# Attention's probabilities turned by VectorE blocks and transfers, a later scan and convolution, and other orders at the seams, in a two-layer hybrid trunk

## The chip, the cores and the metric

The kernel runs on one core of a Trainium2 chip. The metric is the device time of one execution in microseconds, as the median of several runs. The core has a matrix engine (TensorE, PE in the profile, with its weight loads as PEld), VectorE (DVE), ScalarE (ACT), GpSimd (POOL) and SyncE (SP), which issues nearly all transfers here. The engines run side by side and wait for each other by semaphores. Operands lie in SBUF, products in the eight banks of PSUM.

## The reference

Each of two layers computes

```python
x = layer_norm(ALPHA * x + 0.5 * swiglu(x, ffn1...), ln1)
x = layer_norm(ALPHA * x + hybrid_mixer(x, ...), ln2)
x = layer_norm(ALPHA * x + 0.5 * swiglu(x, ffn2...), ln3)
```

on 256 tokens of 1024 features in float32, with 2816 hidden features. The mixer projects `x @ w_in` into the inputs of three branches and their 3 x 1024 gates:

```python
y_conv = (b_g * (conv3(c_g * h) + conv_b)) @ w_br_conv
s      = complex diagonal scan over time of B u;  y = gelu(C s + d u)
y_ssm  = (y * sigmoid(y @ w_glu)) @ w_br_ssm
p      = exp(scores - m) / (sum(exp(scores - m)) + exp(sink - m))   # window of 128
y_attn = (p @ v) @ w_br_attn                   # 8 query heads, 2 key heads, 2 blocks of 128
mix    = (g0 * y_conv + g1 * y_ssm + g2 * y_attn) @ w_out
```

## The kernel before, in words

**Products.** Every large product is made of three: an operand is split into a high part (ScalarE casts it to fp32r) and a low part (VectorE subtracts it), and high by high, high by low and low by high are added up in PSUM. The weights stream through three slots, `raw[0..2]` to `w_hi` and `w_lo`, one chunk of 128x2048 at a time: SP loads chunk k (`load`) once `lo_made` says that chunk k-3 is split, ScalarE makes `w_hi` (`split`), VectorE `w_lo` (`rest`, called `lo(k)` in the mixing stage), and TensorE's `take` waits for `lo_made` and gives the slot back with `used`. All engines follow orders that are written out by hand; there is no scheduler.

**FFN.** Eleven steps of gate and up products and of `down` products (`accumulate`, which adds into four banks: two token tiles by two halves of 512). The hidden rows are turned by `blocks_turned`, a VectorE transpose of 32x32 blocks, four transfers to DRAM and one back that puts the blocks in their places (`turn_hidden` on SP). The last step's hidden rows are turned by TensorE.

**Seams.** At a seam the residual sum, its variance and the normalisation (VectorE, with the power on POOL) of tile 0, then of tile 1 follow the last products; TensorE transposes the tile (`transposes`, 8 pieces), ScalarE scales it out of PSUM and casts it, VectorE subtracts the low part (`x_rest`), and the next stage's first products start on each pair of feature chunks as it is ready (`x_lo`). There are five: into each mixing stage, into each second FFN, and from layer 0 to layer 1. The next stage's first chunks are split ahead: `split_first` and `split_halves` on ScalarE, `rest_first` and `rest_halves` on VectorE. At the seam into the second FFN both halves of the low part stand ahead of the norm; at the other three VectorE makes them inside it. `transposes` of tile 0 stands between the two halves of the last `accumulate`.

**Mixing stage.** TensorE's order is: keys and queries, scores (`S1` for the second block of queries, 256 keys, `S0` for the first, 128 keys), state inputs, and five pairs of gate chunks, `gates_upper(p)` (chunk 9+2p) and `gates_lower(p)` (chunk 10+2p), each half a set of 24 products. Upper products of pair p+1 need the bank that ScalarE's `gate(p, t)` has read. Between them stand:

```python
gates_lower(0); transposes of the probabilities, 24 pieces
gates_upper(1); output_states(0); input_states(1); attend(1); gates_lower(1)
gates_upper(2); gates_lower(2); gates_upper(3); gates_lower(3); gates_upper(4)
attend(0); output_states(1); gates_lower(4)
```

ScalarE normalises the probabilities (`normalise`) and copies the turned ones from six banks to `probsT` (`probs_out`). `input_states` gives B u of a quarter of the states in PSUM, which ScalarE copies (`states`); VectorE turns it (`turn_in`), scans it (`scan`), turns it back (`turn_out`) and TensorE takes it in `output_states`, which needs two quarters. `states(2)` and `turn_in(2)` need `input_states(1)`. VectorE's order from `lo(11)` on is: scan(1), lo(12), turn_out(1), lo(13), convolution (six operations and a product), turn_in(2), lo(14), attn_rest, scan(2), lo(15), turn_out(2), lo(16), turn_in(3), lo(17), scan(3), turn_out(3), lo(18), and then the low parts of the branches.

Line 360 and line 364 issue the blocks' transfers, 334 the weights'; 544 to 546 are gate and up products, 567 `accumulate`, 580 `transposes`, 807 `input_states`, 817 `output_states`, 828 `transpose_probs`, 841 `attend`; 1376 is `rest`, 1413 the block transpose, 1740 to 1772 the turns, 1762 the scan, 1852 to 1857 the convolution, 1153 `gate`, 1161 `states`, 1477 to 1492 the norm, 1388 `rest_halves`.

Of the kernel before, what the change touches and what calls it, by code (L numbers as in the profile page):

```python
# [27 lines left out]
P = 128  # L28
# [71 lines left out]
def trunk(nc, x, ffn1_w_gate, ffn1_w_up, ffn1_w_down, ln1_g, ln1_b, w_in, conv_w, conv_b,  # L100
# [4 lines left out]
    with ctx:  # L105
# [3 lines left out]
        def overlay(first, second):  # L109
# [20 lines left out]
        probsT_first = gates[:, 5, :, :].rearrange("p t (h n) -> p (t h) n", n=P)  # L130
        probsT, rows_hi, rows_lo = overlay(
            [("probsT", [P, 2 * HEADS, P], F32)],
            [("rows_hi", [P, 2, 2, SEQ], F32R), ("rows_lo", [P, 2, 2, SEQ], F32R)])
        S1, y_attn = overlay([("S1", [P, HEADS, 2 * P], F32)], [("y_attn", [P, 4, 2, SEQ], F32R)])

        b_in = S1[:, 0, :].rearrange("p (r t c) -> p r t c", r=2, t=STATE_TILES)
# [57 lines left out]
        ps = ctx.enter_context(nc.psum_tensor("ps", [P, 8, 512], F32))  # L194
        hid_dram = nc.dram_tensor("hid_dram", (4, 32, 4, P), F32, kind="Internal").ap()
# [68 lines left out]
        pT_done = Events(sem("pT_done"), 6)  # L264
        pT_made = Events(sem("pT_made"), 6)
# [45 lines left out]
        def _(sp):  # L311
# [54 lines left out]
            def load_ffn(l, f, w_gate, w_up, w_down, after_two, after_steps, before_last):  # L366
# [14 lines left out]
                after_two()  # L381
                load(l, k0 + 4, rows(w_down, l, 0))

# [53 lines left out]
            for l in range(DEPTH):  # L437
# [18 lines left out]
                def nothing():  # L456
                    pass

                def vectors():

                    dma = sp.dma_start
                    dma(dt_rows[:, :], ssm_log_dt.rearrange("l (t g) -> (l t) g", g=2)).then_inc(small_landed, 16)
# [7 lines left out]
                    for n, v in enumerate((ln1_g, ln1_b, ln2_g, ln2_b, ln3_g, ln3_b)):  # L470
                        dma(ln_rows[16 * n:16 * n + 16, :],
                            v.rearrange("l (c p) -> (l c) p", p=P)).then_inc(small_landed, 16)
# [19 lines left out]
                def norm2():  # L492

                    sp.wait_ge(sum_made.sem, sum_made.at(l, 2))
                    load_norm(l, ln2_g, ln2_b)
# [17 lines left out]
        def _(pe):  # L513
# [43 lines left out]
            def accumulate(slot, buf, start=False, stop=False, tiles=range(NT), halves=((0, 1),)):  # L557
# [104 lines left out]
            def ffn(l, f, norm, turn):  # L662
# [64 lines left out]
                accumulate(2, 1, stop=True, tiles=(1,), halves=((0,),))  # L727
                turn()
                accumulate(2, 1, stop=True, tiles=(1,), halves=((1,),)).then_inc(used.sem, 1)

            for l in range(DEPTH):
# [65 lines left out]
                def input_states(g):  # L797

                    if g:
                        pe.wait_ge(bu_made.sem, bu_made.at(l, 2))  # L800
                        pe.wait_ge(pT_made.sem, pT_made.at(l, 4))
# [19 lines left out]
                def transpose_probs(S, parts, g0):  # L821

                    for g in range(parts):
                        b = (6, 7, 0, 1, 2, 3)[g0 + g]
                        for n in range(4):
                            i = 4 * g + n
                            src = S[:, i // 2, (i % 2) * P:(i % 2) * P + P] if parts == 4 else S[:, i, :]
                            last = nc.tensor.transpose(ps[:, b, n * P:n * P + P], src, ident[:, :])  # L828
                        last.then_inc(pT_done.sem, 1)

                def attend(blk):

                    pe.wait_ge(pT_made.sem, pT_made.at(l, 4 if blk else 6))
                    held = probsT if blk else probsT_first
# [52 lines left out]
                gates_lower(2)  # L887
                gates_upper(3)
# [68 lines left out]
                def output(j, tiles=range(NT), halves=((0, 1),)):  # L957
# [3 lines left out]
                    return accumulate(k % SLOTS, j % 2, start=j == 0, stop=j == 3, tiles=tiles, halves=halves)  # L961
# [17 lines left out]
                output(3, (1,), ((0,),))  # L979
                transposes(l, 1, 0)  # L980
# [5 lines left out]
        def _(sc_):  # L986
# [18 lines left out]
            def split_first(l, stage):  # L1005

                sc_.wait_ge(landed[0], l * LANDED_LAYER[0] + LANDED[K0[stage]])
                hi = kv_w_hi if stage == 1 else first_w_hi
# [31 lines left out]
            def ffn(l, f, ahead):  # L1040
# [901 lines left out]
```

## Time and profile before

| | us |
|---|---|
| median of 3 runs | 1092.29 (1091.78 to 1093.47) |
| profiled execution | 1091.71 |
| its span | 1089.9 |
| TensorE busy | 1078.1 |
| VectorE busy | 762.9 |
| ScalarE busy | 579.7 |

Busy time of TensorE is modelled from pipelined products, so rows overlap: what counts is the distance from one start to the next. An idle note such as "[2.5 <-ACT ...]" in a row says how long an engine stood still before it and whose work it was waiting for. The granted clock of TensorE was 0.997 of full over the span. All times are microseconds from the start of the span.

### The profile page before, as it was taken

The numbers are of one execution on the slowest core, as the hardware profiler recorded it, in microseconds if no ns is written. First come the engines' busy times: TensorE is split into PE (matmuls) and PEld (weight loads), VectorE is DVE, ScalarE is ACT, GpSimd is POOL, SyncE is SP. The second block draws the span as 40 slices with busy tenths as digits, with TensorE's granted clock in tenths as the row PEclk, the third lists the DMA queues.
The fourth block names the chain that finished last, engine by engine and source line by source line (L and its number), as shares of the span: only waits on it lengthen the run. The fifth ranks groups of instructions, "written<-read, shape, count | busy, mean of one in ns | idle before, by whom it ended". The sixth has DMA issues, their size and how long they took to land.

```text
span 1089.9 us, 14539 instructions
## 1 busy us (share of the span) xinstructions
PE 1078.1 (99%) x5329; PEld 894.1 (82%) x5329; DVE 762.9 (70%) x764; ACT 579.7 (53%) x647; POOL 137.2 (13%) x137
## 2 busy tenths in 40 slices
PE   9999999999999999999999999999999999999997
PEld 6788888898888788888878888879988887888885
DVE  5747557789979775555678565676999787755556
ACT  5656654767554544444457555547774546444441
POOL 1398000000000000000006970000000000000000
PEclk9999999999999999999999999999999999999998
DMA  8777778355556477767647777775455574867761
GB/s 282 247 225 233 253 259 213 118 184 170 177 175 206 150 261 232 234 218 265 207 164 243 234 248 234 250 183 175 135 165 162 191 264 133 265 205 240 235 230 42
DMA packets 192369, 226.37 MB, mean 208 GB/s; under 512 B 31540, under 2 KB 157128, under 8 KB 192328
## 3 DMA queue, kind: packets, MB, share of 16 engines
q1 hardware_dynamic: 192328, 225.83, 64.8%
q8 instruction: 26, 0.43, 0.2%
q14 instruction: 15, 0.12, 0.0%
HBM read 214.26 MB, written 11.53 MB: 207 GB/s over the span
## 4 chain that ended last, share of the span: by engine, by line
PE 97%; DMA 1%; issue 1%; DVE 1%; SPq 0%; ACT 0%; POOLq 0%; DVEq 0%; POOL 0%; ACTq 0%
PE ps L567 25%; PE ps L544 19%; PE ps L546 18%; PE ps L545 18%; PE ps L528 2%; PE ps L529 2%; PE ps L530 2%; PE ps L913 1%; PE ps L911 1%; PE ps L912 1%; PE ps L580 1%; PE ps L841 1%; PE ps L828 0%; PE ps L807 0%; DMA xtok<-in_x 0%
## 5 line engine op out<-in xcount | busy, mean ns | idle before, releaser
L1376 DVE TENSOR_TENSOR w_lo<-raw,w_hi 128x2048 fp32r<-128x2048 f32 x173 | 399.7, 2314 | 175.5 <-ACT w_hi L995 174.8
L995 ACT CAST w_hi<-raw 128x2048 fp32r<-128x2048 f32 x173 | 330.1, 1910 | 176.0 <-PE ps L567 80.6
L544 PE MATMUL ps<-w_hi,xT 128*128 128x512 f32 x848 | 331.7, 391 | 0.6 <-DVE w_lo L1388 0.2
L546 PE MATMUL ps<-w_hi,xT 128*128 128x512 f32 x848 | 330.1, 389 | 0.0
L545 PE MATMUL ps<-w_lo,xT 128*128 128x512 f32 x848 | 330.1, 389 | 0.0
L544 PEld LDWEIGHTS ps<-w_hi,xT 128*128 128x128 f32 x848 | 159.2, 188 | 36.6 <-issue 3.6
L546 PEld LDWEIGHTS ps<-w_hi,xT 128*128 128x128 f32 x848 | 159.2, 188 | 33.3
L545 PEld LDWEIGHTS ps<-w_lo,xT 128*128 128x128 f32 x848 | 159.2, 188 | 32.7
L567 PE MATMUL ps<-w_hi,rows_hi 128*128 128x512 f32 x416 | 133.8, 393 | 1.2 <-DVE rows_lo L1419 1.2
L567 PE MATMUL ps<-w_hi,rows_lo 128*128 128x512 f32 x416 | 132.2, 390 | 0.0
L567 PE MATMUL ps<-w_lo,rows_hi 128*128 128x512 f32 x416 | 132.2, 390 | 0.0
L1326 POOL TENSOR_TENSOR rstd<-veps,mhalf 128x1 f32<-128x1 f32 x12 | 8.1, 678 | 782.6 <-DVE veps L1488 782.6
L567 PEld LDWEIGHTS ps<-w_hi,rows_hi 128*128 128x128 f32 x416 | 77.4, 188 | 17.9 <-issue 2.1
L567 PEld LDWEIGHTS ps<-w_hi,rows_lo 128*128 128x128 f32 x416 | 78.1, 188 | 16.6
L567 PEld LDWEIGHTS ps<-w_lo,rows_hi 128*128 128x128 f32 x416 | 78.1, 188 | 15.9
L1014 ACT ACTIVATE act<-ps 128x512 f32<-128x512 f32 (+1 forms) x48 | 27.0, 562 | 95.2 <-PE ps L546 95.1
L1020 ACT CAST rows_hi<-qT 128x512 fp32r<-128x512 f32 x40 | 24.8, 621 | 85.8 <-DMA qT<-hid_dram 85.8
L1405 DVE TENSOR_TENSOR hid<-act,ps 128x512 f32<-128x512 f32 (+1 forms) x48 | 30.7, 640 | 51.9 <-ACT act L1014 51.9
L528 PE MATMUL ps<-xT,w_hi 128*128 128x256 f32 x192 | 54.9, 286 | 0.0
L529 PE MATMUL ps<-xT,w_hi 128*128 128x256 f32 x192 | 54.3, 283 | 0.0
L530 PE MATMUL ps<-xT,w_lo 128*128 128x256 f32 x192 | 54.3, 283 | 0.0
L1419 DVE TENSOR_TENSOR rows_lo<-qT,rows_hi 128x512 fp32r<-128x512 f32 x40 | 29.5, 737 | 34.8 <-ACT rows_hi L1020 34.8
(227 smaller groups left out, 1133.7 us busy)
## 6 DMA issues: line engine op xcount, KB each, us to landing
raw<-in_ffn_w_down SPq DMA_DIRECT2D x44, 1024.0 KB, 5.7
raw<-in_ffn_w_gate SPq DMA_DIRECT2D x86, 512.0 KB, 4.0
raw<-in_ffn_w_up SPq DMA_DIRECT2D x86, 512.0 KB, 5.1
raw<-in_w_in SPq DMA_DIRECT2D x30, 1024.0 KB, 5.2
hid_dram<-qT SPq DMA_DIRECT2D x160, 64.0 KB, 2.4
qT<-hid_dram SPq DMA_DIRECT2D x40, 256.0 KB, 2.7
raw<-in_w_out SPq DMA_DIRECT2D x8, 1024.0 KB, 5.0
raw<-in_w_in SPq DMA_DIRECT2D x8, 512.0 KB, 4.8
```

Source lines behind the costliest of these rows:

```text
L528: mm(o, h[:, c, n], xT[:, c, 0, :], start=i == 0, stop=False)
L529: mm(o, h[:, c, n], xT[:, c, 1, :], start=False, stop=False)
L530: last = mm(o, w[:, c, n], xT[:, c, 0, :], start=False, stop=i == KC - 1)
L544: mm(o, xT[:, c, 0, tok], h, start=c == UPPER_FIRST[0], stop=False, skip_group_check=True)
L545: mm(o, xT[:, c, 0, tok], w, start=False, stop=False, skip_group_check=True)
L546: return mm(o, xT[:, c, 1, tok], h, start=False, stop=c == UPPER_FIRST[-1], skip_group_check=True)
L567: last = mm(acc[:, t, n, :], left[:, buf, c, tok], right[:, c, n * 512:n * 512 + 512], start=start and first and c == 0, stop=stop and lef ...
L995: nc.scalar.copy(w_hi[s][:, :], raw[s][:, :]).then_inc(hi_made.sem, 1)
L1014: act_(act[:, tiles, :], ps[:, bank + tiles.start:bank + tiles.stop, 0:256], ACT.Silu).then_inc(silu_made.sem, 1)
L1376: tt(w_lo[s][:, :], raw[s][:, :], f32(w_hi[s][:, :]), ALU.subtract).then_inc(lo_made.sem, 1)
L1405: tt(hid[:, :, :].rearrange("p m (t n) -> p t m n", t=NT)[:, tiles], act[:, tiles, :].rearrange("p t (m n) -> p t m n", m=2), ps[:, bank + ...
L1419: tt(rows_lo[:, 0].rearrange("p m (t a j) -> p (m t) a j", t=NT, a=4), hid_by_row, f32(rows_hi[:, 0]).rearrange("p m (t a j) -> p (m t) a ...
```

## The change

The probabilities are no longer transposed by TensorE. VectorE turns 32x32 blocks of `S1` and `S0` (`probs_blocks`, one instruction each of 128x2048 and 128x1024), SP writes them to DRAM in four transfers each (256 and 128 KB apiece) and reads them back in one each (1 MB and 512 KB), in the order `probs_out(1)`, then after two more loads `probs_out(0)`, `probs_back(1)`, `probs_back(0)`. `attend` waits for the transfer. TensorE's order becomes gates upper and lower 0 and 1, then the states, gates 2, `attend(1)`, gates 3. The convolution moves behind `lo(16)` and `attn_rest` behind `lo(17)` on VectorE. At the seams, `transposes` of tile 0 moves three products earlier, and at the three seams of the other kind the low parts of the next weights are made ahead of the norm. Of the small loads at the start, six move behind the first `w_down`.

```diff
+            def probs_out(l, blk):
+                src = blocks_second if blk else blocks_first
+                sp.wait_ge(pblocks_made.sem, pblocks_made.at(l, 2 - blk))
+                for a in range(4):
+                    sp.dma_start(probs_dram[blk].rearrange("g i a r -> a i g r")[a],
+                                 src[32 * a:32 * a + 32, :].rearrange("i (g r) -> i g r", g=4)
+                                 ).then_inc(pblocks_out[blk].sem, 16)
+            def probs_back(l, blk):
+                sp.wait_ge(pblocks_out[blk].sem, pblocks_out[blk].at(l, 1))
+                sp.dma_start(turned_second if blk else turned_first,
+                             probs_dram[blk].rearrange("g i a r -> (g i) (a r)")).then_inc(probs_turned[blk].sem, 16)
...
-                after_two()
+                small(0)
                 load(l, k0 + 4, rows(w_down, l, 0))
+                small(1)
...
                     load(l, MIX0 + PAIR0 + 2 * p, gate_pair(l, p, 1))
-                    load(l, MIX0 + PAIR0 + 2 * p + 1, gate_pair(l, p, 0))
                     if p == 3:
+                        probs_out(l, 0)
+                        probs_back(l, 1)
+                        probs_back(l, 0)
+                        load(l, MIX0 + PAIR0 + 2 * p + 1, gate_pair(l, p, 0))
+                    else:
+                        load(l, MIX0 + PAIR0 + 2 * p + 1, gate_pair(l, p, 0))
+                    if p == 2:
+                        probs_out(l, 1)
+                    if p == 4:
                         sp.wait_ge(yc_made.sem, yc_made.at(l, 1))
...
+                            if between and c == 0:
+                                between()
...
-                accumulate(2, 1, stop=True, tiles=(1,), halves=((0,),))
-                turn()
+                accumulate(2, 1, stop=True, tiles=(1,), halves=((0,),), between=turn)
...
                 gates_lower(0)
-                pe.wait_ge(bu_made.sem, bu_made.at(l, 2))
-                pe.wait_ge(probs_made.sem, probs_made.at(l, 1))
-                transpose_probs(S1, 4, 0)
-                pe.wait_ge(probs_made.sem, probs_made.at(l, 2))
-                transpose_probs(S0, 2, 4)
                 gates_upper(1)
-                pe.wait_ge(pT_made.sem, pT_made.at(l, 6))
+                gates_lower(1)
                 output_states(0)
                 input_states(1)
-                attend(1)
-                gates_lower(1)
                 gates_upper(2)
                 gates_lower(2)
+                attend(1)
                 gates_upper(3)
...
                 split(l, k0 + FFN_CHUNKS - 1)
+                if following:
+                    split_first(*following)
                 silu(l, s0 + STEPS, (half_used.sem, half_used.at(l, f + 1)), 4, slice(0, 1))
                 silu(l, s0 + STEPS + 1, pair(k0 + FFN_CHUNKS - 3), 4, slice(1, 2))
                 last_hidden_hi(l, 2 * f + 1, 0, 6)
-                ahead()
+                if following:
+                    split_halves(*following)
                 last_hidden_hi(l, 2 * f + 2, 1, 7)
...
-                probs_out(0, 4)
-                probs_out(4, 2)
                 split(l, MIX0 + 13)
+                gate(1, 0)
+                gate(1, 1)
                 states(2)
-                attn_hi(1, 1)
                 split(l, MIX0 + 14)
                 states(3)
-                gate(1, 0)
-                gate(1, 1)
                 split(l, MIX0 + 15)
                 split(l, MIX0 + 16)
+                sc_.wait_ge(pblocks_out[1].sem, pblocks_out[1].at(l, 1))
                 gate(2, 0)
                 gate(2, 1)
+                attn_hi(1, 1)
                 split(l, MIX0 + 17)
...
+                def last_tiles():
+                    hidden(l, s0 + STEPS + 1, 4, slice(1, 2))
+                    last_hidden_lo(l, s0 + STEPS, 0, 6)
+                if following:
+                    rest_first(*following, last_tiles)
+                    second = rest_halves(*following)
+                    second(0)
+                    second(1)
...
-                rest_first(l, 1)
-                norm(l, 0, MIX0 - 1, 0.5, rest_halves(l, 1), gap=second_tile)
+                norm(l, 0, MIX0 - 1, 0.5, lambda lower: None, gap=second_tile)
...
+                def probs_blocks(S, out, blk):
+                    dve.wait_ge(probs_made.sem, probs_made.at(l, 2 - blk))
+                    nc.vector.transpose(out.rearrange("p (g k j) -> p g k j", g=4, j=32),
+                                        S[:, :, :].rearrange("p h (b g j) -> p g (h b) j", g=4, j=32)
+                                        ).then_inc(pblocks_made.sem, 1)
...
                 scan(1)
+                probs_blocks(S1, blocks_second, 1)
                 lo(12)
                 turn_out(1)
+                probs_blocks(S0, blocks_first, 0)
                 lo(13)
+                turn_in(2)
+                lo(14)
+                scan(2)
+                lo(15)
+                turn_out(2)
+                lo(16)
                 dve.wait_ge(cz_made.sem, cz_made.at(l, 1))
...
                 tt(cv_h[:, :, :], cv_c[:, :, :], cv_b[:, :, :], ALU.mult).then_inc(yc_made.sem, 1)
-                turn_in(2)
-                lo(14)
-                attn_rest(1, 1)
-                scan(2)
-                lo(15)
-                turn_out(2)
-                lo(16)
                 turn_in(3)
                 lo(17)
+                attn_rest(1, 1)
                 scan(3)
```

## Rows read from the trace of the kernel before

**Rows 1.** Page parts 1 and 4: busy time; chain that ended last, by engine.
```profile
PE 1078.1 (99%) x5329; PEld 894.1 (82%) x5329; DVE 762.9 (70%) x764; ACT 579.7 (53%) x647; POOL 137.2 (13%) x137
...
PE 97%; DMA 1%; issue 1%; DVE 1%; SPq 0%; ACT 0%; POOLq 0%; DVEq 0%; POOL 0%; ACTq 0%
```

**Rows 2.** The chain in order of time: start, us, what.
```profile
48.71 5.44 PE ps L567 x24
...
261.32 2.62 PE ps L828 x24
269.40 1.00 PE ps L817 x16
270.40 1.08 PE ps L807 x16
```

**Rows 3.** Timeline of TensorE, mixing stage of layer 0: start, us, what.
```profile
261.16 2.78 PE L828 MATMUL ps<-ident,S 128*128 128x128 f32 x24
...
308.23 0.50 PE L544 MATMUL ps<-w_hi,xT 128*128 128x512 f32 x1
```

**Rows 4.** Timeline of VectorE, mixing stage of layer 0.
```profile
262.15 2.27 DVE L1376 TENSOR_TENSOR w_lo<-raw,w_hi 128x2048 fp32r<-128x2048 f32 x1
264.33 1.22 DVE L1740 TENSOR_TENSOR td<-bu,rot_c 128x1024 f32<-128x1024 f32 x1
...
270.13 0.41 DVE L1852 TENSOR_SCALAR cv_c<-cv_z,cw_cur,cb_cur 128x256 f32<-128x256 f32 x1
...
273.71 1.22 DVE L1740 TENSOR_TENSOR td<-bu,rot_c 128x1024 f32<-128x1024 f32 x1
...
277.43 2.29 DVE L1376 TENSOR_TENSOR w_lo<-raw,w_hi 128x2048 fp32r<-128x2048 f32 x1
279.64 0.68 DVE L1784 TENSOR_TENSOR y_attn<-ps,y_attn 128x512 fp32r<-128x512 f32 x1
280.24 2.43 DVE L1762 TENSOR_TENSOR_SCAN bu<-st_cur,sw 128x256 f32<-128x256 f32 x4
...
302.57 2.28 DVE L1376 TENSOR_TENSOR w_lo<-raw,w_hi 128x2048 fp32r<-128x2048 f32 x1
```

**Rows 5.** The block transposes of line 1413: ns min/median/max, first and last start.
```profile
L1413 DVE STREAM_TRANSPOSE qT<-hid x40: 711/712/716, 21.2 to 1055.4; 128x512 f32<-128x512 f32 x40
```

**Rows 6.** Timeline of ScalarE, mixing stage of layer 0.
```profile
261.02 1.05 ACT L1153 ACTIVATE gates<-ps 128x512 f32<-128x512 f32 x2
...
271.54 1.01 ACT L1161 COPY bu<-ps 128x1024 f32<-128x1024 f32 x1 [4.77 <-PE ps L807]
```

**Rows 7.** Timeline of VectorE at the seam into layer 0's mixing stage.
```profile
187.18 0.15 DVE L1488 TENSOR_SCALAR veps<-mv 128x1 f32<-128x1 f32 x1
...
187.58 1.22 DVE L1388 TENSOR_TENSOR w_lo<-raw,w_hi 128x1024 fp32r<-128x1024 f32 x1
188.71 1.00 DVE L1492 TENSOR_SCALAR xtok<-xtok,mv,rstd 128x512 f32<-128x512 f32 x2
```

**Rows 8.** Timeline of VectorE at the seam into layer 0's second FFN.
```profile
358.43 1.00 DVE L1492 TENSOR_SCALAR xtok<-xtok,mv,rstd 128x512 f32<-128x512 f32 x2 [0.67 <-POOL rstd L1326]
```

**Rows 9.** Timeline of TensorE, transposes of tiles 0 and 1 at these seams.
```profile
189.31 1.11 PE L580 MATMUL ps<-ident,xtok 128*128 128x128 f32 x8
...
196.70 1.11 PE L580 MATMUL ps<-ident,xtok 128*128 128x128 f32 x8
...
359.68 1.04 PE L580 MATMUL ps<-ident,xtok 128*128 128x128 f32 x8
```

**Rows 10.** Timeline of TensorE at the first `down` of the kernel.
```profile
32.10 0.70 PE L567 MATMUL ps<-w_hi,rows_hi 128*128 128x512 f32 x2 [1.17 <-DVE rows_lo L1419]
```

**Rows 11.** Timeline of SP at the start; window table, last columns clock, DMA share, GB/s.
```profile
17.51 0.39 SPq L334 DMA_DIRECT2D raw<-in_ffn_w_down  x1
...
18.00:19.00 1.00, 1.00 (x7) 0.81 (x6) 1.00 (x1) 0.00 (x0) 0.00 (x0) 1.00 0.66 84
```

**Rows 12.** The chain at the start: the hidden blocks on their way to DRAM.
```profile
24.08 3.82 DMA hid_dram<-qT
```

More of the change, by code:

```diff
@@ L194, in trunk @@
         ps = ctx.enter_context(nc.psum_tensor("ps", [P, 8, 512], F32))
+        probs_dram = [nc.dram_tensor(f"probs_dram{n}", (4, 32, 4, n * HEADS * 32), F32, kind="Internal").ap()
+                      for n in (1, 2)]
         hid_dram = nc.dram_tensor("hid_dram", (4, 32, 4, P), F32, kind="Internal").ap()
@@ L263, in trunk @@
         probs_made = Events(sem("probs_made"), 2)
-        pT_done = Events(sem("pT_done"), 6)
-        pT_made = Events(sem("pT_made"), 6)
+        pblocks_made = Events(sem("pblocks_made"), 2)
+        pblocks_out = [Events(sem(f"pblocks_out{n}"), 1, unit=64) for n in range(2)]
+        probs_turned = [Events(sem(f"probs_turned{n}"), 1, unit=16) for n in range(2)]
         pv_done = Events(sem("pv_done"), 2)
@@ L454, in norm1, with nothing, vectors @@
                     load_norm(l, ln1_g, ln1_b)
-                def nothing():
+                def nothing(part=0):
                     pass
-                def vectors():
+                def vectors(part):
                     dma = sp.dma_start
+                    if part:
+                        for n, v in enumerate((ln1_g, ln1_b, ln2_g, ln2_b, ln3_g, ln3_b)):
+                            dma(ln_rows[16 * n:16 * n + 16, :],
+                                v.rearrange("l (c p) -> (l c) p", p=P)).then_inc(small_landed, 16)
+                        return
                     dma(dt_rows[:, :], ssm_log_dt.rearrange("l (t g) -> (l t) g", g=2)).then_inc(small_landed, 16)
@@ L490, in _, with norm2 @@
                     load(l, MIX0 + OUT[j], rows(w_out, l, 256 * j))
-                def norm2():
+                def norm2(part):
+                    if part:
+                        return
                     sp.wait_ge(sum_made.sem, sum_made.at(l, 2))
@@ L555, in first_gate_up, with accumulate @@
                     last.then_inc(used.sem, 1)
-            def accumulate(slot, buf, start=False, stop=False, tiles=range(NT), halves=((0, 1),)):
+            def accumulate(slot, buf, start=False, stop=False, tiles=range(NT), halves=((0, 1),), between=None):
                 h, w = wide(w_hi[slot]), wide(w_lo[slot])
@@ L819, in output_states @@
                     last.then_inc(c_done.sem, 1)
[L821 to L829, printed above, removed]
                 def attend(blk):
-                    pe.wait_ge(pT_made.sem, pT_made.at(l, 4 if blk else 6))
-                    held = probsT if blk else probsT_first
+                    pe.wait_ge(probs_turned[blk].sem, probs_turned[blk].at(l, 1))
+                    held = (turned_second if blk else turned_first).rearrange("p (a k j) -> p k a j", a=4, j=32)
                     for m in range(4):
@@ L955, in turn_sums, with output @@
                         last.then_inc(sT_done.sem, 1)
-                def output(j, tiles=range(NT), halves=((0, 1),)):
+                def output(j, tiles=range(NT), halves=((0, 1),), between=None):
                     k = MIX0 + OUT[j]
@@ L960, in output @@
                     pe.wait_ge(sum_lo.sem, sum_lo.at(l, max(j, 1) + 1))
-                    return accumulate(k % SLOTS, j % 2, start=j == 0, stop=j == 3, tiles=tiles, halves=halves)
+                    return accumulate(k % SLOTS, j % 2, start=j == 0, stop=j == 3, tiles=tiles, halves=halves,
+                                      between=between)
                 attention(0)
@@ L1007, in split_first @@
                 sc_.wait_ge(landed[0], l * LANDED_LAYER[0] + LANDED[K0[stage]])
+                if stage == 1:
+                    sc_.wait_ge(bblk_made.sem, bblk_made.at(l, 1))
                 hi = kv_w_hi if stage == 1 else first_w_hi
@@ L1038, in discretise, with ffn @@
                 act_(sc[:, 3, :], sc[:, 2, :], ACT.Sin, scale=0.5).then_inc(state_act.sem, 1)
-            def ffn(l, f, ahead):
+            def ffn(l, f, following=None):
                 k0, s0, b0 = FFN0[f], f * (STEPS + 1), f * (STEPS - 1)
@@ L1132, in _ @@
                     turn_input()
-                ffn(l, 0, lambda: split_first(l, 1))
-                split_halves(l, 1)
+                ffn(l, 0, (l, 1))
                 norm(l, 0)
@@ L1168, in normalise @@
                     last.then_inc(probs_made.sem, 1)
-                def probs_out(g0, n):
-                    for g in range(g0, g0 + n):
-                        sc_.wait_ge(pT_done.sem, pT_done.at(l, g + 1))
-                        b = (6, 7, 0, 1, 2, 3)[g]
-                        held, i = (probsT_first if g0 else probsT), 4 * (g - g0)
-                        nc.scalar.copy(held[:, i:i + 4, :], ps[:, b, :].rearrange("p (c n) -> p c n", c=4)
-                                       ).then_inc(pT_made.sem, 1)
                 def attn_hi(n, blk):
                     sc_.wait_ge(pv_done.sem, pv_done.at(l, n))
+                    if blk:
+                        sc_.wait_ge(pblocks_out[0].sem, pblocks_out[0].at(l, 1))
                     nc.scalar.copy(y_attn[:, :, 0, blk * P:blk * P + P], ps[:, 3, :].rearrange("p (m q) -> p m q", m=4)
@@ L1260, in _ @@
                 gate(3, 1)
+                sc_.wait_ge(yc_made.sem, yc_made.at(l, 1))
+                nc.scalar.copy(y_cs[:, 0:2, 0, :], cv_h[:, :, :]).then_inc(yc_hi.sem, 1)
                 split(l, MIX0 + 19)
```

33 lines of the change are left out of this document (14 added, 19 removed).

## Prediction

> **What bounds the kernel now.** First I read the engine totals and the chain that ended last. TensorE is busy for 1078.1 of 1089.9 us and its work is 97% of the chain [rows 1]. The long products run back to back: 24 of them take 5.44 us, 0.227 us each [rows 2]. So only two things move the time: TensorE work added or taken away, and stretches in which TensorE stands still. The profiled execution took 1091.71 us, 1.81 us more than its span; the median of the runs shown is 0.58 us above it. I make the sum in microseconds of difference and put it on the median of 1092.29. About 0.2% (2.2 us) is what a measurement of this kernel can tell from no change.
>
> Next I read VectorE in the mixing stage. From 262.15 to 304.85 us its rows follow each other with no idle note: weight remainders (`lo`), turns, scans, the convolution [rows 4]. TensorE does not feel it, because the last remainder of that run, `lo(18)`, ends at 304.85 and `gates_lower(4)` starts at 308.23 [rows 3, 4]: a cover of 3.4 us, all there is.
>
> **TensorE's transposes go.** 24 transposes of probabilities take 2.62 us in a layer [rows 2]: 5.24 us for two layers, all on the chain. The six ScalarE copies out of PSUM go too; ScalarE does not bound there. `attend(1)` only moves, its products are the same.
>
> **VectorE's blocks come.** No row shows a stream transpose of 128x2048 or 128x1024. The nearest: 128x512 takes 0.71 us in all of 40 cases [rows 5], a two-input operation on 128x2048 occupies 2.2 us from start to start, one on 128x1024 about 1.15 [rows 4]. Lower bound for the two: 3.3 us a layer; upper bound 4 and 2 times the 0.71, 4.3 us. I take 3.4, since one long instruction pays its fixed part once.
>
> **Mixing stage, walked in the clock of the old layer 0.** `gates_lower(0)` ends at 261.16 [rows 2, 3], and `gates_upper(1)` now follows at once. It needs the bank that `gate(0, 0)` reads, and on ScalarE that gate starts at 261.02, behind the normalisation, one half of a pair of 1.05 us [rows 6]. With 0.15 us from release to product (as at the first `down`, below) the products start at 261.8: a stall of 0.6 that the transposes used to fill. `gates_upper(1)` and `gates_lower(1)` take 10.9, to 272.7; `output_states(0)` and `input_states(1)` 2.1 more [rows 2], to 274.9. The copy `states(2)` starts within 0.1 and takes 1.0 [rows 6]: VectorE can start `turn_in(2)` at 276.0.
>
> VectorE meanwhile: blocks of S1 from 262.15 (2.2), `lo(12)` 2.2, `turn_out(1)` 3.6, blocks of S0 1.2, `lo(13)` 2.2 [rows 4], free at 273.6. `lo(12)` is ready at 266.7, before TensorE's 267.2. Then VectorE stands idle for 2.4 us, because the convolution, which filled this place, has moved. `lo(14)` is queued behind `turn_in(2)`, and TensorE has only `gates_upper(2)` (5.4, to 280.4) before it needs it: 276.0 + 3.7 + 2.3 = 282.0, a stall of about 1.8. From there VectorE is the bound: `turn_in(2)` 3.72, `lo(14)` 2.21, `scan(2)` 2.4, `lo(15)` 2.2, `turn_out(2)` 3.60, `lo(16)` 2.2, convolution 3.58, `turn_in(3)` 3.72, `lo(17)` 2.2, `attn_rest` 0.60, `scan(3)` 2.4, `turn_out(3)` 3.6, `lo(18)` 2.28, together 34.7, to 310.7. Each is a distance between two starts, or the duration of the scan and of the last remainder [rows 4]; `turn_out` is the 5.80 from 264.33 to 270.13 less the one `lo` in it. `gates_lower(4)` starts at 310.8, 2.6 us **later** than its 308.23, though 2.6 us of TensorE work are gone. The stalls add up to 5.2: 0.6 + 1.8 + about 1.4 before `gates_upper(4)` + 1.4 before `gates_lower(4)`. Behind this TensorE again waits for gelu and gates at the old distances. Two layers: **+5.2**.
>
> What the wait of `probs_out` and `probs_back` on SP holds back: the weights of `gates_lower(3)`, and `w_glu` and all behind it for the convolution. The first can be issued at about 277 (blocks out at 276 if they take the 3.8 us of the hidden ones [rows 12]), needs some 5 us to land and 2 to split, and is wanted on VectorE at 290: 6 us of cover, cost nothing. The second is issued at 296 and wanted for `lo(19)` at 312. `attend(1)` needs its turned blocks at 287.6, some 13 us after SP sends for them. By the Trainium skill (VectorE: DVE Perf Modes, The three transpose paths) VectorE's transpose makes 32x32 blocks only, and its rules leave a 128x128 transpose to TensorE where PSUM will do. No row here weighs the whole path against 2.62 us; the idle and block times above are what it costs in this kernel, so by that rule the sum has the same sign.
>
> **Seams.** In three of the five seams the second half of the weight remainder (1.22 us at 187.58) lies between the variance and the normalisation, which so starts at 188.71 [rows 7]. At the other kind VectorE waits only for POOL, 0.67 us [rows 8]: the variance ready at 187.33 plus 0.67 gives 188.0, 0.7 earlier. The transposes of tile 0 start at 189.31, the moment tile 0 is there; three products earlier is 188.6, where the new upper half is ready: a wait of about 0.1. At the other two seams the upper half is normalised at about 358.97 (half of the row at 358.43), so the transposes can start at 359.0 instead of 359.68 [rows 8, 9]. From there the chain evacuation, split, remainder, variance of tile 1, its transposes (196.70, 7.4 later [rows 9]) moves up by the same 0.65, while TensorE has the same work to do in between; so the small waits it makes in this chain vanish. On ScalarE `split_first` now stands ahead of the two last silus, where it idles today, so I cost it at nothing; without that cover it would be up to its 1.9 us. Bounds 0 and 0.8; I take 0.62 a seam: **-3.1**.
>
> **Start.** TensorE waits 1.17 us at 32.10 for the first hidden rows [rows 10], which came late out of DRAM behind weights. The first `w_down` load was issued at 17.51, behind twelve small ones, and DMA moved only 84 GB/s from 18 to 19 us [rows 11]. Six of the twelve now follow it, so it starts 2.7 us earlier and the queue is 1.2 us shorter when the hidden blocks come. Bounds 0 and 1.3; I take **-1.1**.
>
> Sum: +5.2 - 3.1 - 1.1 = +1.0; 1092.71 for an execution like the profiled one, **1093.3** on the median. TensorE's removed work is in the +5.2 already.
>
> **The rivals.**
> Cover holds (faster). If VectorE kept ahead of TensorE, nothing but removals would be left: -5.2 - 3.1 - 1.1, 1082.9. Against it stand the 3.4 us of cover and the idle place behind `lo(13)`; it needs 5 us of VectorE time that I don't see.
> Blocks are dear (slower). A stream transpose with its far strides at half rate costs 6.8 instead of 3.4 a layer. All of it lies on VectorE's chain: +3.4 twice, 1100. It decides as soon as both transposes together take over 4.6 us a layer (1095.7). Against it: the 0.71 of 128x512, which reads in blocks as well.
> Seams and start bring nothing: another wait in the same chain (tile 1's variance, or SP) takes the place. +5.2 alone, 1097.5.
> Blocks travel slowly. The skill (same page and section) warns that a copy which transposes by strides is 19 times slower than the crossbar's. Here the runs are of 1 to 2 KB. From rows: the four 64 KB transfers of the hidden blocks end in one of 3.82 us in the chain [rows 12]. At four times the bytes and that rate the blocks of S1 would need 15 us, those of S0 another 7.6 behind them, out at 287; the weights of `gates_lower(3)` queued behind them on SP would land at 292, and their remainder, due on VectorE at 290, would come 4 us late: +4 twice, 1101. It decides from some 16 us for both.
> That the change does not do what it says is hardly possible for the transposes, which are simply not issued.
>
> **How the numbers follow.** Forecast (VectorE bounds, seams give) 0.60, its own range 1090.5 to 1096; of it 0.10 falls under 1090.1 and 0.07 above 1094.5. Cover holds or mostly holds: 0.13. Dear blocks 0.10, no gain at seams or start 0.14, slow transfers 0.03. Faster by over 0.2% 0.23, within 0.43, slower 0.34. Range 1088.5 to 1098.5: it leaves out full cover and dear blocks, about 0.2.
>
> **What would show it.** TensorE rows: idle before `gates_lower(2)`, `gates_upper(4)` and `gates_lower(4)` put down to VectorE's w_lo; `gates_lower(4)` starts about 49.6 us after `gates_lower(0)` ends instead of 47.1. VectorE: stream transposes of 2.3 and 1.2 us, an idle of 2.4 before `turn_in(2)` put down to ScalarE's bu. Seams: transposes of tile 1 still 7.4 us after those of tile 0, but with three more products between them and hardly a gap. Start: no idle at the first `down`. I am wrong if `turn_in(2)` starts without idle, if a transpose takes over 3 us, or if ScalarE or SP turns up as releaser in TensorE's idle.

## The result

The changed kernel takes 1093.84 us (median of 20 runs, 1092.18 to 1096.38), the kernel before 1092.47 (20 runs, 1091.48 to 1094.75) measured beside it. The ratio is 1.0013, with a 95% interval of 1.0007 to 1.0019: slower by about 1.4 us, measurable but inside the 0.2% that the prediction called no change. The profiled execution took 1093.41 us with a span of 1091.6.

### The profile page after: what moved, and what is told of

It is laid out like the page before. It is cut to its first block, busy times and chain, and to the rows that moved or that the text cites. A ratio compares the mean times of both kernels' runs of the same rounds, so it can differ in the third digit from the quotient of the medians.

```text
span 1091.6 us, 14455 instructions
## 1 busy us (share of the span) xinstructions
PE 1072.6 (98%) x5281; PEld 888.9 (81%) x5281; DVE 771.7 (71%) x768; ACT 573.7 (53%) x635; POOL 132.7 (12%) x137
## 4 chain that ended last, share of the span: by engine, by line
PE 82%; DVE 8%; ACT 3%; DMA 3%; issue 2%; SPq 2%; POOLq 0%; DVEq 0%; POOL 0%; ACTq 0%
PE ps L601 23%; PE ps L578 15%; PE ps L580 15%; PE ps L579 15%; DVE w_lo L1390 3%; PE ps L562 2%; PE ps L563 2%; PE ps L564 2%; DMA hid_dram<-qT 2%; PE ps L931 1%; PE ps L929 1%; PE ps L930 1%; ACT w_hi L1013 1%; ACT S L1189 1%; PE ps L616 1%
```

## The profile after

The page's part 1, and from part 4 the chain that ended last by engine, answer to [rows 1]:

```profile
PE 1072.6 (98%) x5281; PEld 888.9 (81%) x5281; DVE 771.7 (71%) x768; ACT 573.7 (53%) x635; POOL 132.7 (12%) x137
...
PE 82%; DVE 8%; ACT 3%; DMA 3%; issue 2%; SPq 2%; POOLq 0%; DVEq 0%; POOL 0%; ACTq 0%
```

TensorE has 5.5 us less to do, and a longer span. Its share of the chain fell from 97 to 82%: part of the time is now set by VectorE. The waits of TensorE over the whole kernel (who waited for whom: us in total, times, longest) name the place:

```profile
PE ps L578 <- DVE w_lo L1390: 7.5, 6, 1.6
...
PE ps L578 <- ACT gates L1175: 0.8, 2, 0.4
```

In the timeline of TensorE, mixing stage of layer 0, these waits are four rows: in front of `gates_upper(1)`, `gates_lower(2)`, `gates_upper(4)` and `gates_lower(4)`. The last answers to the 308.23 of [rows 3].

```profile
260.47 0.47 PE L578 MATMUL ps<-w_hi,xT 128*128 128x512 f32 x1 [0.41 <-ACT gates L1175]
...
280.96 0.50 PE L578 MATMUL ps<-w_hi,xT 128*128 128x512 f32 x1 [1.59 <-DVE w_lo L1390]
...
300.81 0.50 PE L578 MATMUL ps<-w_hi,xT 128*128 128x512 f32 x1 [1.10 <-DVE w_lo L1390]
...
309.68 0.50 PE L578 MATMUL ps<-w_hi,xT 128*128 128x512 f32 x1 [1.07 <-DVE w_lo L1390]
```

The timeline of VectorE beside them answers to [rows 4] and [rows 5]: the two block transposes (L1808), `lo(13)`, `turn_in(2)` with its idle, `lo(14)`, the convolution, `turn_in(3)`, and `lo(18)`.

```profile
260.88 2.29 DVE L1808 STREAM_TRANSPOSE gates<-S 128x2048 f32<-128x2048 f32 x1
...
268.86 1.24 DVE L1808 STREAM_TRANSPOSE S<-S 128x1024 f32<-128x1024 f32 x1
270.02 2.25 DVE L1390 TENSOR_TENSOR w_lo<-raw,w_hi 128x2048 fp32r<-128x2048 f32 x1
274.89 1.23 DVE L1764 TENSOR_TENSOR td<-bu,rot_c 128x1024 f32<-128x1024 f32 x1 [2.62 <-ACT bu L1183]
...
278.62 2.29 DVE L1390 TENSOR_TENSOR w_lo<-raw,w_hi 128x2048 fp32r<-128x2048 f32 x1
...
291.16 0.41 DVE L1891 TENSOR_SCALAR cv_c<-cv_z,cw_cur,cb_cur 128x256 f32<-128x256 f32 x1
...
294.74 1.22 DVE L1764 TENSOR_TENSOR td<-bu,rot_c 128x1024 f32<-128x1024 f32 x1
...
307.34 2.29 DVE L1390 TENSOR_TENSOR w_lo<-raw,w_hi 128x2048 fp32r<-128x2048 f32 x1
```

From 274.89 on no row has an idle note: VectorE works without a gap until `lo(18)` ends at 309.63, and TensorE starts `gates_lower(4)` 0.05 later.

Where the time went, as distances between starts of the same TensorE instructions in the two traces:

| stretch | before | after | change |
|---|---|---|---|
| product on the input at 10.84 (after: 11.28) to the first `down` | 21.26 | 19.94 | -1.32 |
| first `down` to the last `down` of that FFN | 150.14 | 150.55 | +0.41 |
| five seams (three from last `down` to projection or next `down`, two into the second FFN) | 157.63 | 154.15 | -3.48 |
| layer 0, projection to `gates_lower(4)` | 102.77 | 105.49 | +2.72 |
| layer 1, the same | 102.78 | 105.50 | +2.72 |

The table adds up to +1.05, the two spans differ by 1.7. What is left, 0.65 us, lies in the later arrival of the input in this execution (0.44, ahead of the first stretch) and in single products (0.2). At the seam into layer 0's mixing stage the rows that answer to [rows 7] and [rows 9] are, VectorE's normalisation:

```profile
186.62 0.15 DVE L1513 TENSOR_SCALAR veps<-mv 128x1 f32<-128x1 f32 x1
...
187.44 1.00 DVE L1517 TENSOR_SCALAR xtok<-xtok,mv,rstd 128x512 f32<-128x512 f32 x2 [0.34 <-POOL rstd L1340]
```

and TensorE's transposes of tiles 0 and 1 there, and of tile 0 at the next seam:

```profile
188.04 1.11 PE L616 MATMUL ps<-ident,xtok 128*128 128x128 f32 x8
...
195.44 1.12 PE L616 MATMUL ps<-ident,xtok 128*128 128x128 f32 x8
...
360.50 1.11 PE L616 MATMUL ps<-ident,xtok 128*128 128x128 f32 x8
```

The normalisation starts 0.82 after the variance instead of 1.53, and the two transposes are 7.40 apart as before, with three more products between them.

## The experiments

Every ratio is to the kernel before on the same chip. Medians of the kernel before in the three series: 1092.53, 1091.90 and 1092.06.

### The parts alone

`seams_start` is the kernel before with the seams and the start of the change, and nothing of the mixing stage.

```diff
-                accumulate(2, 1, stop=True, tiles=(1,), halves=((0,),))
-                turn()
+                accumulate(2, 1, stop=True, tiles=(1,), halves=((0,),), between=turn)
...
-                rest_first(l, 1)
-                norm(l, 0, MIX0 - 1, 0.5, rest_halves(l, 1), gap=second_tile)
+                norm(l, 0, MIX0 - 1, 0.5, lambda lower: None, gap=second_tile)
```

> The old mixing stage with the new seams and the new start. My theory (the parts add up, each seam gives 0.57 to 0.83 us by the distances in the trace of the changed kernel, 3.5 for five, the start 0.9 net): 4.4 us under the kernel before, 1088.1. Rival (the seams gain only because the mixing stage before them changed, or the start's gain is noise): within 1 us of the kernel before, 1091.5 to 1092.5.

Measured: 1088.91 us (6 runs, 1087.53 to 1089.98), ratio 0.9965 (0.9953 to 0.9977), 3.6 us less. Its mixing stage takes 102.79 us, as in the kernel before, so the gain does not come from the new mixing stage; conversely the mixing stage's edits cost about 4.9 us (1093.84 against 1088.91), 5.4 by the distances above. The median is 0.8 above the expected 1088.1. Its trace shows something that the changed kernel's does not, in the timeline of TensorE at the seam from layer 0 to layer 1:

```profile
532.89 0.44 PE L691 MATMUL ps<-ident,hid 128*128 128x128 f32 x2 [1.63 <-DVE hid L1414]
```

and in ScalarE's timeline just before:

```profile
530.20 1.90 ACT L1017 CAST first_w_hi<-raw 128x2048 fp32r<-128x2048 f32 x1 [2.02 <-DMA raw<-in_ffn_w_up]
532.00 0.65 ACT L1022 ACTIVATE act<-ps 128x256 f32<-128x256 f32 x2
```

`split_first` waited 2.0 us for its weights to land, and the two silus queued behind it on ScalarE came late for TensorE. Two experiments below had it too. It comes and goes between executions of the same work: at the first seam, up to which the changed kernel, `s0_twice` and `lo14_ahead` issue the same instructions, ScalarE waited 0, 0.88 and 1.60 us in front of `split_first`. In the changed kernel and in `lo14_ahead` SP issues the last 1 MB of `w_down` at 161.41 and 161.33; it lands after 4.8 us in the one and 8.1 in the other, the last transfer of the hidden blocks lands 2.5 later with it, and SP, which waits for that transfer, issues the next stage's first weights at 168.2 and at 170.7.

`start_only` moves only the six small loads.

```diff
-                after_two()
+                after_two(0)
                 load(l, k0 + 4, rows(w_down, l, 0))
+                after_two(1)
```

> The kernel before with only the six small loads behind the first w_down. Theory: the 1.17 us in front of the first down goes, some of it comes back at the later steps (0.4 in the changed kernel's trace): 0.9 us less, 1091.6. Rival: the whole 1.3 stays, 1091.2, or all of it comes back before the first seam, 1092.5.

Measured: 1091.48 us (11 runs), ratio 0.9994 (0.9985 to 1.0003), 1.05 us less by the medians but not apart from nothing by the interval. The trace says where: the first stretch of the table above, up to the first `down`, takes 20.24 us instead of 21.26, and no idle instead of 1.17 [rows 10] there. In the other nine traces with this start the distance is 19.92 to 20.93. In two of them an idle in front of the first `down` is back (0.72 in `conv_in_gap`, 0.80 in `seams_silu`), in three a stop of 0.3 to 0.7 stands near 26 us instead. The changed kernel's 19.94 is at the good end; against the one trace of the kernel before, the start gives from 0.3 to 1.3 us.

### What the block transposes cost

`s0_twice` makes VectorE's transpose of S0 twice in the changed kernel.

```diff
+                    if not blk:
+                        again = S1[:, 4:8, :].rearrange("p h n -> p (h n)")
+                        nc.vector.transpose(again.rearrange("p (g k j) -> p g k j", g=4, j=32),
+                                            S[:, :, :].rearrange("p h (b g j) -> p g (h b) j", g=4, j=32))
```

> The changed kernel, with the block transpose of S0 (1.24 us in the trace) made twice, the first time into unused columns of S1. What is computed stays the same. Theory: VectorE has 2.6 us of idle behind lo(13) while it waits for states(2), so a block transpose in front of it costs nothing: same as the changed kernel, 1093.8. Rival, as I priced it in the prediction (all of the block time lies on VectorE's chain): 1.16 us a layer, 2.3 more, 1096.1.

Measured: 1093.67 us (11 runs), ratio 1.0009 (0.9997 to 1.0022): as the changed kernel's 1.0013. Its VectorE rows show where the 1.16 us went:

```profile
269.24 1.24 DVE L1810 STREAM_TRANSPOSE S<-S 128x1024 f32<-128x1024 f32 x1
270.40 1.20 DVE L1812 STREAM_TRANSPOSE S<-S 128x1024 f32<-128x1024 f32 x1
271.53 2.25 DVE L1390 TENSOR_TENSOR w_lo<-raw,w_hi 128x2048 fp32r<-128x2048 f32 x1
275.27 1.23 DVE L1764 TENSOR_TENSOR td<-bu,rot_c 128x1024 f32<-128x1024 f32 x1 [1.50 <-ACT bu L1183]
```

The idle in front of `turn_in(2)` shrank from 2.62 to 1.50. The 1.16 us ahead of that idle were free; what lies behind it sets the end of `lo(18)`. That work is free up to the whole 2.62 is what one expects from this, and `lo14_ahead`, next, puts 2.2 us there.

### Filling the idle

`lo14_ahead` puts the remainder of `gates_lower(2)` into it.

```diff
                 split(l, MIX0 + 13)
+                split(l, MIX0 + 14)
                 gate(1, 0)
                 gate(1, 1)
                 states(2)
-                split(l, MIX0 + 14)
...
+                lo(14)
                 turn_in(2)
-                lo(14)
                 scan(2)
```

> The changed kernel with split(14) ahead of the gates and states(2) on ScalarE and lo(14) ahead of turn_in(2) on VectorE, so that a remainder fills the idle behind lo(13). Theory (VectorE's chain from turn_in(2) to lo(18) bounds the stage): 2.2 us less a layer, 4.4 in all, 1089.4; the stall in front of gates_lower(2) is gone and the one in front of gates_lower(4) smaller. Rival (weights of gates_lower(3), which landed at 284.6 after the probabilities' transfers, become the bound): only the 1.75 us stall moves on, 1093 or more.

Measured: 1089.34 us (6 runs, 1088.63 to 1092.19), ratio 0.9975 (0.9963 to 0.9987), 4.5 us under the changed kernel where 4.4 were expected. Projection to `gates_lower(4)` takes 103.27 us in layer 0: 2.22 less, and 103.42 in layer 1. The stall in front of `gates_lower(4)` did not get smaller (1.10), the one in front of `gates_upper(4)` did (0.79). The landing of the weights behind the probabilities' transfers, the rival, shows in layer 1, in the rows of ScalarE and TensorE:

```profile
822.77 1.91 ACT L1013 CAST w_hi<-raw 128x2048 fp32r<-128x2048 f32 x1 [7.42 <-DMA raw<-in_w_in]
...
825.31 0.47 PE L578 MATMUL ps<-w_hi,xT 128*128 128x512 f32 x1 [0.77 <-ACT gates L1175]
```

ScalarE waited for the weights of `gates_lower(3)`, and the gates queued behind them came 0.77 us late for `gates_upper(3)`. The stall in front of `gates_upper(4)` there is 0.12 instead of 0.79, so the late landing took the place of another stall and cost 0.15 us. The same stands in layer 0 of `orders`, below, with 0.41. The profiled execution, at 1092.19 the slowest of the six, had the late `split_first` of above twice (0.9 and 0.7 us of TensorE idle).

`conv_in_gap` instead puts the convolution (from its wait for `cz_made` to the product `cv_h`) back behind `lo(13)`.

```diff
                 lo(13)
+                dve.wait_ge(cz_made.sem, cz_made.at(l, 1))
...
+                tt(cv_h[:, :, :], cv_c[:, :, :], cv_b[:, :, :], ALU.mult).then_inc(yc_made.sem, 1)
                 turn_in(2)
                 lo(14)
                 scan(2)
                 lo(15)
                 turn_out(2)
                 lo(16)
-                dve.wait_ge(cz_made.sem, cz_made.at(l, 1))
...
-                tt(cv_h[:, :, :], cv_c[:, :, :], cv_b[:, :, :], ALU.mult).then_inc(yc_made.sem, 1)
                 turn_in(3)
```

> The changed kernel with the convolution back at its old place on VectorE, behind lo(13). Theory: its 3.6 us fill the idle of 2.6 and push turn_in(2) by 1.0, so lo(18) ends 2.6 us earlier in each layer, or 2.4 if the remainder of gates_lower(3) waits for its landing: 4.8 to 5.2 us less than the changed kernel, 1088.6 to 1089.0. Rival (stall in front of gates_lower(2) decides, which grows by 1.0): 2 us more, 1095.8.

Measured: 1092.51 us (11 runs, 1090.06 to 1094.95), ratio 1.0005 (0.9996 to 1.0015). The theory missed by 3.5 us or more, for two reasons. First, I had followed VectorE alone: `lo(18)` is indeed early enough that TensorE no longer waits for it, but the stall in front of `gates_lower(2)`, 2.44 us instead of 1.59, is then on TensorE's own path. In layer 1 the stage takes 103.75 us, 1.75 less than in the changed kernel, not 2.4. Second, in layer 0 it takes 105.39, and there the windows of this kernel show why (us, busy per engine, then granted clock, DMA share, GB/s):

```profile
280.00:283.00 3.00, 0.56 (x3) 0.47 (x3) 2.96 (x4) 0.00 (x0) 0.00 (x0) 1.00 0.87 326
283.00:286.00 3.00, 3.00 (x10) 2.33 (x10) 3.00 (x5) 0.92 (x1) 0.00 (x0) 0.63 0.82 244
286.00:290.00 4.00, 4.00 (x19) 2.99 (x19) 3.97 (x5) 1.69 (x3) 0.00 (x0) 0.85 0.63 207
```

In front of them TensorE had stood still, in its timeline:

```profile
282.48 0.50 PE L578 MATMUL ps<-w_hi,xT 128*128 128x512 f32 x1 [2.44 <-DVE w_lo L1390]
```

TensorE took up its work at 282.48, and from 283.77 to 287.19 the granted clock was half, 1.2 GHz, instead of full, 2.4 GHz. Two of its rows in that stretch:

```profile
284.18 0.63 PE L578 MATMUL ps<-w_hi,xT 128*128 128x512 f32 x1
284.60 0.63 PE L579 MATMUL ps<-w_lo,xT 128*128 128x512 f32 x1
```

Eight products in a row took 0.41 to 0.43 us from start to start instead of 0.227, which is 1.6 us lost. The same stall in layer 1 of the same execution was followed by full clock. Without any fall both layers would give 1093.84 - 2 x 1.75 = 1090.3, and the fastest run is 1090.06; with one or two falls 1092 and 1094, where the others lie. (The kernel before is 0.6 lower in this series, which these sums leave out.) That the runs that were not profiled had falls is argued from their times, not shown.

### Other orders, and the convolution late

`orders` is `lo14_ahead` with two more moves on ScalarE.

```diff
+                states(1)
                 gate_first(GT, ps[:, 4, :].rearrange("p (t n) -> p t n", t=NT), gates[:, 0, :, SEQ:2 * SEQ])
                 split(l, MIX0 + 11)
-                states(1)
...
                 split(l, MIX0 + 12)
-                normalise(S0, 0)
                 gate(0, 0)
+                normalise(S0, 0)
                 gate(0, 1)
```

> lo14_ahead and two more orders on ScalarE: gate(0, 0) ahead of the normalisation of S0, states(1) ahead of the first-columns gate. Theory: the 0.57 us stall in front of gates_upper(1) goes and takes states(2) and the whole chain with it: 2.8 us less a layer than the changed kernel, 1088.2. Rival: VectorE is saturated before that and the 0.57 is only moved: 1089.4, as lo14_ahead.

Measured: 1088.87 us (6 runs), ratio 0.9969 (0.9957 to 0.9982). The stage takes 102.57 and 102.58 us, 2.92 less than in the changed kernel, 0.7 more than `lo14_ahead` gained in layer 0: the stall of 0.57 in front of `gates_upper(1)` is gone, and it came on top as expected. The median is 0.7 above the expected one; the late `split_first` stood twice in its trace (0.4 and 0.75 us).

`late_conv` takes the convolution out of the stretch in which VectorE bounds.

```diff
-        cv_b, w_glu = overlay([("cv_b", [P, 2, SEQ], F32)], [("w_glu", [P, 2, 256], F32)])
+        cv_b = sb("cv_b", [P, 2, SEQ])
+        w_glu = S0[:, 0:4, :].rearrange("p (c a) n -> p c (a n)", c=2)
...
-                        sp.wait_ge(yc_made.sem, yc_made.at(l, 1))
...
                 lo(16)
-                dve.wait_ge(cz_made.sem, cz_made.at(l, 1))
...
-                tt(cv_h[:, :, :], cv_c[:, :, :], cv_b[:, :, :], ALU.mult).then_inc(yc_made.sem, 1)
                 turn_in(3)
...
                 lo(19)
+                dve.wait_ge(cz_made.sem, cz_made.at(l, 1))
...
+                tt(cv_h[:, :, :], cv_c[:, :, :], cv_b[:, :, :], ALU.mult).then_inc(yc_made.sem, 1)
                 lo(20)
+                dve.wait_ge(yc_hi.sem, yc_hi.at(l, 1))
+                tt(y_cs[:, 0:2, 1, :], cv_h[:, :, :], f32(y_cs[:, 0:2, 0, :]), ALU.subtract).then_inc(yc_lo.sem, 1)
```

> orders, and the convolution behind lo(19) on VectorE, its high part behind gate(4, 1) on ScalarE, w_glu in a part of S0 so that its load waits no more for the convolution. Theory: VectorE's 3.6 us leave the stretch in which it bounds, lo(18) is ready before TensorE asks, all stalls of the stage go: 5.3 us a layer less than the changed kernel, 1083.2, 9.2 under the kernel before. Rival: the convolution's low part now comes late for its branch products, or other work of VectorE behind lo(18) does: 1086 to 1090 with TensorE idle in front of the branches.

Measured: 1084.88 us (5 runs, 1083.39 to 1085.62), ratio 0.9935 (0.9921 to 0.9948). It beats both kernels. The stage takes 100.31 us in layer 0, 5.18 less than in the changed kernel, and between 255 and 320 us no row of TensorE has an idle note. `lo(18)` ends at 302.54, and `gates_lower(4)` starts at 303.92. VectorE's rows there show a gap behind `lo(18)`, the first behind `turn_in(2)`, and the convolution in its new place:

```profile
300.26 2.28 DVE L1390 TENSOR_TENSOR w_lo<-raw,w_hi 128x2048 fp32r<-128x2048 f32 x1
303.66 0.69 DVE L1815 TENSOR_TENSOR y_attn<-ps,y_attn 128x512 fp32r<-128x512 f32 x1 [1.11 <-ACT y_attn L1196]
304.26 0.86 DVE L1897 SCALAR_TENSOR_TENSOR td<-uT,d_cur,ps 128x256 f32<-128x256 f32 x2
305.05 2.29 DVE L1390 TENSOR_TENSOR w_lo<-raw,w_hi 128x2048 fp32r<-128x2048 f32 x1
307.25 0.41 DVE L1905 TENSOR_SCALAR cv_c<-cv_z,cw_cur,cb_cur 128x256 f32<-128x256 f32 x1
```

### The late silu

`late_conv_silu` and `seams_silu` are `late_conv` and `seams_start` with one move in ScalarE's FFN.

```diff
                 split(l, k0 + FFN_CHUNKS - 1)
-                if following:
-                    split_first(*following)
                 silu(l, s0 + STEPS, (half_used.sem, half_used.at(l, f + 1)), 4, slice(0, 1))
+                if following:
+                    split_first(*following)
                 silu(l, s0 + STEPS + 1, pair(k0 + FFN_CHUNKS - 3), 4, slice(1, 2))
```

> late_conv with split_first between the last two silus on ScalarE instead of ahead of both. In the traces of seams_start, lo14_ahead and orders, split_first waited 1.1 to 2.0 us for weights to land and held up the silu behind it, so that TensorE stood still 0.4 to 1.6 us in front of its transposes of the last hidden rows; the profiled late_conv had no such wait and took 1083.4, its median is 1084.9. Theory: that wait is now off TensorE's path, median down to 1083.4 to 1084.0, ratio to the kernel before near 0.9922. Rival (the spread has another cause, or the later split_first delays VectorE in the seam): 1084.9 or more.

Measured: 1083.58 us (5 runs, 1082.69 to 1084.77), ratio 0.9923 (0.9909 to 0.9937), on the expected value, 8.5 us under the kernel before: the fastest version. All waits of TensorE that its profile lists are at the kernel's start:

```profile
PE ps L641 <- POOL zero_b L1320: 1.3, 1, 1.3
PE ps L647 <- DMA xtok<-in_x: 0.7, 1, 0.7
PE ps L578 <- DVE w_lo L1402: 0.2, 1, 0.2
```

Its interval overlaps that of `late_conv`, so the 0.0012 between them goes the expected way but is not shown. Nor does the trace show that the move is the cause: `split_first` waited 0.14 us at most for its weights there, so this execution had no late landing to cover.

> seams_start with the same one move. Theory: 1088.1 instead of 1088.9, no idle of TensorE in front of the transposes of the last hidden rows. Rival: 1088.9 or more.

Measured: 1088.63 us (5 runs, 1087.27 to 1089.67), ratio 0.9962 (0.9948 to 0.9976) against 0.9965 of `seams_start`: inconclusive. The idle in front of the last hidden rows is gone from its trace, but here too `split_first` had hardly to wait (0.13 at most). The profiled execution stood 1.3 us at the start waiting for the input and 0.80 and 0.32 in front of two `down`, which comes from elsewhere.

## Why the prediction was right

**The mixing stage, +5.2 forecast, +5.44 by the distances.** The walk held nearly row by row. From the end of `gates_lower(0)` to `gates_lower(4)` 49.6 us were forecast; after is 309.68 less 259.90, 49.8. The excess in front of `gates_upper(1)` was put at 0.6 and is 0.57, in front of `gates_lower(2)` 1.8 and 1.75, in front of `gates_upper(4)` 1.4 and 1.27, in front of `gates_lower(4)` 1.4 and 1.14. Together that is 4.73, not 5.2. The removed transposes are 2.54 from start to start (261.16 to 263.70 before), and 0.5 us that the sum did not have made up for the smaller stalls: where TensorE starts a new run of products, the first ones are further apart (0.34, then 0.23 to 0.24 behind 280.96 instead of 0.227), and a run that ends in other work costs 0.32; there are five such runs now instead of two. So the total is closer than its terms. VectorE's idle in front of `turn_in(2)` was put at 2.4 and is 2.62, with ScalarE's copy as the releaser. `lo14_ahead`, `orders` and `late_conv` each removed what the walk says they should: the bound is VectorE's chain behind `states(2)`. One sign of being wrong was worded against the prediction itself: ScalarE was not to turn up as a releaser in TensorE's idle, but the stall of 0.6 in front of `gates_upper(1)` waits for ScalarE's gate, as forecast, and the list of waits has it (0.8 us, two times).

**The blocks, 3.4 a layer forecast.** 2.29 and 1.24 us, 3.4 from start to start: the 0.71 of 128x512 [rows 5] scales like a two-input operation. But the rival of dear blocks was priced wrongly. I laid all extra block time on VectorE's chain; `s0_twice` shows that 1.16 us more behind `lo(12)` cost nothing, with 1.50 of idle still left. The wrong step in that rival is to price added work without looking for the next idle behind it, which I had worked out myself a paragraph earlier.

**The seams, -3.1 forecast, -3.5.** The mechanism is as told: the normalisation 0.7 earlier at three seams, the transposes three products earlier at all five, 0.57 to 0.83 each. `seams_start` confirms the sign without the new mixing stage, and the size within 1 us. The cost of nothing for `split_first` was too simple. The profiled execution of the changed kernel paid none, but it holds only while the next weights have landed in time, and where they had not (`seams_start`, `lo14_ahead`, `orders`) it cost 0.4 to 1.6 us, within the 1.9 that the prediction named for the case.

**The start, -1.1 forecast.** -1.32 to the first `down`, of which 0.4 came back during the rest of that FFN, where TensorE waited for turned hidden rows again (a row at 96.96 with 0.27 of idle): net -0.9. Luck has a part in this term: in the other traces the same start gave 0.3 to 1.3 by this distance, and `start_only` alone is not clear of noise.

**SP's queue, nothing forecast.** Right in the cost, off in the size of the cover. (Between `probs_out(1)` and `probs_out(0)` stands one load, not two as told above.) The blocks went out in 6.5 and 5.8 us, 12.3 for both, the second by 275.93, where the prediction had 276: so the rival of slow transfers, which needed 16, did not come. The weights of `gates_lower(3)` were issued at 276.40 but landed after 8.2 us, not 5. ScalarE's rows:

```profile
284.58 1.92 ACT L1013 CAST w_hi<-raw 128x2048 fp32r<-128x2048 f32 x1 [5.26 <-DMA raw<-in_w_in]
286.40 1.07 ACT L1175 ACTIVATE gates<-ps 128x512 f32<-128x512 f32 x2
```

The split ends at 286.50 and the remainder starts at 288.95, so about 2.4 us of cover were left, not 6. On the path that the prediction did not look at it was less: the gates that queue behind this split end at 287.47, 1.1 us before `gates_upper(3)` at 288.53. This was the nearest thing to a second bound, and in `lo14_ahead` and `orders` it became visible.

The errors were small and of both signs: +0.24, -0.4 and +0.2 in these terms, 0.4 from the arrival of the input and 0.2 in single products. They make the 0.7 by which the two profiled executions lie further apart than the +1.0 of the sum; the median lies 0.5 from its forecast. That it is so close owes something to errors that cancel.

Of the rivals, cover did not hold (it would have given 1083), and the point from which it holds now lies between two runs. By the rows of `late_conv` `lo(18)` had to end about 5 us earlier in a layer than in the changed kernel; with the 2.9 of `orders` the stalls are still there, and in `late_conv` it ends 6.5 earlier, 1.4 before TensorE asks. By the Trainium skill (VectorE: DVE Perf Modes, Rules for kernel authors) a 128x128 transpose belongs on TensorE where PSUM will do. For the change as made that comes out right, but with `late_conv` the blocks pay: a ratio of 0.9935 against 0.9965 for `seams_start`, which keeps the transposes on TensorE. The stage takes 100.31 us against 102.79, 2.48 less, about the 2.54 that the transposes took. No run pairs the transposes on TensorE with the later convolution; that stage of `seams_start` has no idle of TensorE to remove, so nothing should be gained there. The path is not what cost the time; the place of the other work was.

## What to carry to other kernels

Where one engine runs through without a gap and another keeps just ahead of it, taking work off the bound engine uses up the cover of its follower, and what goes beyond the cover has to be taken off the follower between the same two waits. Here the cover was 3.4 us; 2.6 us off TensorE met 3.4 us more and 2.6 us of new idle on VectorE, 5.2 too much. Before moving an operation out of a place, ask which wait it was covering: the convolution covered the round trip through `input_states` and `states`. Price added work from the next idle of its engine, and follow both engines to the later one, since removing one stall can leave a longer one on the other path.

## What the runs showed of the hardware that was not expected

In `conv_in_gap` TensorE stopped for 2.44 us in both layers. In layer 0 it worked again for 1.3 us, and then the granted clock was half for 3.4 us (products 0.41 to 0.43 instead of 0.227 us apart); in layer 1 of the same execution it stayed full. In the ten other traces no stop behind the start is longer than 1.63 us, and the clock is full from about 7 us to the last products. The fall cost 1.6 us on top of the stall itself. Whether it comes in every execution is not shown; the times of the others speak for none, one or two of them.

A load of 1 MB that is issued at the same place of the same work can land 3.3 us later in one execution than in another (4.8 and 8.1 us, `w_down` ahead of the first seam), and it delays what SP issues behind the transfers that land with it.
